# Dilated attention heads: tiles by distance (neighbours in natural order, every fourth token by class) in place of tiles by parity

## The reference, cut to what matters

```python
DILATED_CONFIGS = ((128, 1), (512, 4), (2048, 16))   # (window, dilation)
def dilated_window_branch(q, k, v, slopes, window, dilation):
    # Query t attends keys t + dilation*j, j in [-R, R], R = window // (2*dilation)
    ...
    s = s - slopes[:, None, None] * dist[None]          # dist = |query - key|
    s = jnp.where(valid[None, :, None, None], s, NEG_INF)
    m = jnp.max(s, axis=-1); p = jnp.exp(s - m[..., None]); z = jnp.sum(p, axis=-1)
    ...
wts = jnp.exp(m_all - jnp.max(m_all, axis=0, keepdims=True))
z = jnp.sum(z_all * wts, axis=0)
o_a = jnp.sum(o_all * wts[..., None], axis=0) / z[..., None]
```

## Time and profile before

| | us |
|---|---|
| median of 3 runs | 2054.36 (2050.83 to 2055.28) |
| the profiled execution, its own time | 2054.35 |
| its span, first to last instruction | 2052.6 |
| PE busy | 2016.1 |
| DVE busy | 1211.8 |
| ACT busy | 1129.9 |
| POOL busy | 953.4 |

### The profile page before, as it was taken

The page is one execution under the profiler, slowest core; times in us unless marked ns, Lnnn a source line. Parts: engine busy times, 40 slices in busy tenths (PEclk is TensorE's granted clock), DMA queues, the critical chain, the costliest instruction groups (busy, mean ns, idle before and its releaser), DMA issues.

```text
span 2052.6 us, 25510 instructions
## 1 busy us (share of the span) xinstructions
PE 2016.1 (98%) x9456; PEld 1621.0 (79%) x9456; DVE 1211.8 (59%) x1941; ACT 1129.9 (55%) x1440; POOL 953.4 (46%) x487
## 2 busy tenths in 40 slices
PE   8999998999999999999999999999999999999998
PEld 6788886888888877777887777888777777777888
DVE  6632145325776666673559777414577778776454
ACT  6242234435666666665446444344677778888431
POOL 1222224435555555556102666433566676677401
PEclk9999998999999999999999999999999999999999
DMA  5133478617665754633435333362323343332534
GB/s 203 66 119 126 151 258 310 169 67 155 130 118 109 177 118 93 158 83 122 153 108 163 131 124 116 103 195 78 87 58 85 75 121 74 80 77 90 169 105 167
DMA packets 172143, 261.38 MB, mean 127 GB/s; under 512 B 78754, under 2 KB 89634, under 8 KB 172020
## 3 DMA queue, kind: packets, MB, share of 16 engines
q1 hardware_dynamic: 172020, 259.76, 44.6%
HBM read 161.78 MB, written 97.92 MB: 127 GB/s over the span
## 4 chain that ended last, share of the span: by engine, by line
PE 90%; ACT 3%; DVE 2%; DMA 2%; issue 1%; POOL 1%; SPq 0%; DVEq 0%; ACTq 0%
PE SA L1966 13%; PE OP L2012 11%; PE SM L1892 5%; PE SA L546 5%; PE OP L2019 5%; PE OP L546 5%; PE SM L2065 5%; PE OP L1104 4%; PE SA L2065 4%; PE SA L1104 4%; PE OS L2012 3%; PE OS L546 2%; PE OS L1104 2%; PE OS L2065 2%; PE SM L1888 2%; PE OS L2019 1%
## 5 line engine op out<-in xcount | busy, mean ns | idle before, releaser
L2486 POOL TENSOR_TENSOR c_PL<-c_PF,c_PH 128x1024 fp32r<-128x1024 f32 x128 | 307.7, 2407 | 137.6 <-ACT c_PH L2188 79.9
L2486 POOL TENSOR_TENSOR ab_PL<-ab_PF,ab_PH 128x1024 fp32r<-128x1024 f32 (+3 forms) x128 | 264.7, 2068 | 192.3 <-ACT ab_PH L2188 135.8
L2185 ACT ACTIVATE ab_PF<-SA 128x1024 f32<-128x1024 f32 (+3 forms) x160 | 143.7, 898 | 157.9 <-PE SA L1927 84.7
L2185 ACT ACTIVATE c_PF<-SA 128x1024 f32<-128x1024 f32 x160 | 164.6, 1029 | 84.4 <-PE SA L1966 83.0
L2273 DVE TENSOR_REDUCE c_MH<-SM 128x1 f32<-128x512 f32 x256 | 171.0, 684 | 66.4 <-PE SM L1892 66.3
L437 POOL TENSOR_TENSOR e_wl<-e_raw,e_wh 128x1024 fp32r<-128x1024 f32 (+1 forms) x30 | 70.6, 2354 | 185.1 <-ACT e_wh L613 185.1
L2188 ACT ACTIVATE c_PH<-c_PF 128x1024 fp32r<-128x1024 f32 x128 | 136.0, 1063 | 4.1
L1966 PE MATMUL SA<-c_Q,c_KA 128*128 128x512 f32 x320 | 127.8, 399 | 3.4 <-ACT c_PF L2185 3.4
L1966 PE MATMUL SA<-c_Q,c_KB 72*128 72x512 f32 x320 | 127.1, 397 | 0.0
L1036 POOL TENSOR_TENSOR n_wl<-n_raw,n_wh 128x1024 fp32r<-128x1024 f32 (+1 forms) x24 | 54.5, 2271 | 153.9 <-ACT n_wh L1201 153.9
L1892 PE MATMUL SM<-c_KA,c_Q 128*128 128x512 f32 x320 | 125.1, 392 | 0.0
(11 more groups left out here) (555 smaller groups left out, 5909.5 us busy)
## 6 DMA issues: line engine op xcount, KB each, us to landing
c_Q<-qC_hi SPq DMA_DIRECT2D x32, 384.0 KB, 5.0
e_raw<-in_w_tiles SPq DMA_DIRECT2D x20, 512.0 KB, 4.1
n_raw<-in_w_tiles SPq DMA_DIRECT2D x20, 512.0 KB, 3.7
e_XF<-in_xT SPq DMA_DIRECT2D x12, 512.0 KB, 10.6
silu_gate<-e_ta SPq DMA_DIRECT2D x24, 256.0 KB, 2.0
ab_Q<-qA_hi SPq DMA_DIRECT2D x16, 384.0 KB, 5.4
ab_G<-silu_gate SPq DMA_DIRECT2D x24, 256.0 KB, 3.7
ab_res<-in_xT SPq DMA_DIRECT2D x24, 256.0 KB, 2.9
```

Source lines behind the costliest of these rows:

```text
L2185: nc.scalar.activation(used(PF[p], h, s), used(SA, h, s), ACT.Exp).then_inc(e_done, 1)
L2486: nc.gpsimd.tensor_tensor(used(PL[p], h, s), used(PF[p], h, s), used(PH[p], h, s).bitcast(F32), ALU.subtract).then_inc(p_lo[0], 1)
```

## The change

In a dilated head, keys are held in two kinds of tiles. A class tile has 128 keys of one residue modulo 4 (`class_keys`, `class_queries`: columns of the same `Q1`, `KA`, `Q3`, `KB` buffers with a step of 4 elements, 16 bytes) against all 256 queries of that residue (sample: 128). A near tile has 128 neighbouring keys in natural order against the queries within 64 of them, 192 or 256 columns. A pair is now taken in both tiles if it is held by both kinds of window, so no logarithm is needed, and one bias table of 640 columns in one part does; pairs held by both strided windows are counted by doubling their exponentials on DVE (`doubled`, a product with a table of ones and twos), between the exponential and the copy on ACT. A tile has six score matmuls instead of seven. The values are kept in class order (`VV`) and in natural order (`VN`), low part, high part and ones side by side; the product of a near tile reads `PH` and `PL` with a step of 4 elements, so that the sums stand by class, and for the prompt it is cut in two halves. All copies to `PH` of these heads are ACT's, all subtractions POOL's. The maximum units are 12 a head, of two matmuls and two DVE reductions each; the near maxima are brought into class order by four small matmuls with selection matrices (`pick_max`) and taken together with the class maxima by four small DVE operations (`both_near`), for sample and prompt. The projections store q and k in natural order and the values with 4 KB rows.

```diff
-    def pair_scores(h, s, x, q1, q3, ka, kb):
...
-            nc.tensor.matmul(o, k1, side_of(q1, side, sample), start=True, stop=False, skip_group_check=True)
-            nc.tensor.matmul(o, ident[:], own_bias(Bhi[h % 3], m, n), start=False, stop=False,
-                             skip_group_check=True)
-            nc.tensor.matmul(o[:, l0:l1], ident[:], low, start=False, stop=False, skip_group_check=True)
...
+    def class_keys(t, i):
+        o = i // CLASSES * CH + i % CLASSES
+        return t[:, o:o + CLASSES * (P - 1) + 1:CLASSES]
+
+    def class_queries(t, i, sample):
+        o = SEQ if sample else 0
+        n = (DEC if sample else SEQ) // CLASSES
+        o += i % CLASSES
+        return t[:, o:o + CLASSES * (n - 1) + 1:CLASSES]
...
+            add(c, class_keys(ka, t), class_queries(q1, t, sample), start=True)
+            add(d, tile_keys(ka, i, sample), tile_queries(q1, i, sample))
+            add(c, ident[:], class_bias(Bhi[h % 3], t, sample))
+            add(d, ident[:], near_bias(Bhi[h % 3], i, sample))
+            add(c, class_keys(kb[0:na], t), class_queries(q3[0:na], t, sample), stop=True)
+            return add(d, tile_keys(kb[0:na], i, sample), tile_queries(q3[0:na], i, sample), stop=True)
...
+                nc.tensor.matmul(SM[:, o:o + n], class_keys(q, t), class_queries(k, t, sample), start=True, stop=True)
+                nc.tensor.matmul(SM[:, o + n:o + n + w], tile_keys(q, i, sample), tile_queries(k, i, sample),
+                                 start=True, stop=True).then_inc(m_ready, 1)
...
+                    for b in range(1 if sample else 2):
+                        rs = slice(0, CLASSES) if sample else slice(2 * b, 2 * b + 2)
+                        yield (of_classes(PH[p][:, d])[:, rs], of_classes(PL[p][:, d])[:, rs], near_v,
+                               by_class(out[:])[:, rs, u0:u1], s == 2 and b == 1, False)
...
-            if s not in SLOW_HI:
+            if s not in SLOW_HI or h < NA:
+                if h < NA:
+                    act.wait_ge(p_twice, g + 1)
                 act.wait_ge(e_done, g + 1)
                 nc.scalar.activation(used(PH[p], h, s), used(PF[p], h, s), ACT.Copy).then_inc(p_hi[0], 1)
...
+        def doubled(g):
+
+            h, s, p = g // NS, g % NS, PF[g % 4]
+            dve.wait_ge(e_done, g + 1)
+            if s < 2:
+                x = p[:].rearrange("p (x n) -> p x n", x=2)[:, :, 0:P]
+                count = twice[:, 64:64 + P].unsqueeze(1).to_broadcast([P, 2, P])
+            else:
+                u0 = 64 * ((s - 2) // CLASSES)
+                x, count = p[:, u0:u0 + 192], twice[:, 64 - u0:64 - u0 + 192]
+            nc.vector.tensor_tensor(x, x, count, ALU.mult).then_inc(p_twice, 1)
...
+                for m in range(0, TT, CLASSES):
+                    rows = values[m:m + CLASSES].rearrange("t p d -> (t p) d")
+                    sp.dma_start(VV[b][:, m:m + CLASSES, 0:2 * HD].bitcast(F32),
+                                 rows.rearrange("(u r) d -> u r d", r=CLASSES)).then_inc(in_v[b], 16)
```

More of the change, by code:

```diff
@@ L347, in store @@
                 sp.wait_ge(acc_read, n + 1)
+            if name in ("value", "vB"):
+                for r in (slice(0, HD), slice(HD, P)):
+                    sp.dma_start(S["vA" if name == "value" else "vB"][c, r],
+                                 sv[stage_of(i)][r].rearrange("p h x d -> p h (x d)")).then_inc(stored[stage_of(i)], 16)
+                return
             for part, st in (("hi", sh), ("lo", sl)):
                 src = st[stage_of(i)][rows(n), :]
[L350 to L355, removed]
+                if name == "rope key":
                     dst = S["krB", part][:, cols(c)]
@@ L385, in sync @@
                 sp.wait_ge(tok_ready, 16)
[L386 to L390, removed]
+                sp.dma_start(rtok[:], S["tok0"].rearrange("o (i p) -> (o p) i", p=P),
+                             allow_slow_non_contiguous=True).then_inc(tok_done, 16)
             for w in begins[n]:
@@ L1893, in max_unit, with pick_max @@
                              start=True, stop=True).then_inc(m_ready, 1)
+        def pick_max(h, prompt):
+            pe.wait_ge(m_done, unit0[h + 1] if prompt else unit0[h] + NQ)
+            wait_count(pe, aug_done, 2 * h + prompt)
+            n, o = (NP, 0) if prompt else (NQ, NP)
+            for r in range(CLASSES):
+                mm = nc.tensor.matmul(MT[:, 256 + 8 * r:256 + 8 * r + n], pick[:, r, :], MN[:, o:o + n], start=True,
+                                      stop=True)
+            mm.then_inc(mt_ready, 1)
         def transpose_max(h, prompt):
@@ L2008, in pv @@
             on, n_hi = hi_at[g]
             pe.wait_ge(p_hi[on], n_hi)
-            for pc, kt, out, st, en in halves():
-                for i, (w, r) in enumerate(((vh, P), (vl, HD))):
-                    nc.tensor.matmul(out[0:r], w[:, kt, :], PH[p][:, pc], start=(st and i == 0), stop=False,
-                                     skip_group_check=h < NA)
+            for ph, _, v, out, st, en in halves():
+                for i, (w, r) in enumerate(((v[:, HD:3 * HD], P), (v[:, 0:HD], HD))):
+                    nc.tensor.matmul(out[0:r], w, ph, start=(st and i == 0), stop=False, skip_group_check=h < NA)
@@ L2025, in between @@
                 max_unit(0, u)
+            if NA and g in (sample_at - 1, prompt_at - 1) and part == 2:
+                pe.wait_ge(const_set, n_set)
+                pick_max(0, g == prompt_at - 1)
             if g in (sample_at, prompt_at) and part == 2:
@@ L2033, in tensor @@
             units = units_of(h + 1, s) if h + 1 < NH else ()
-            some = len(units) // 2
+            some = (len(units) + 1) // 2
             scores(h, s)
+            if s in (2, NS - 1) and h + 1 < NA:
+                pick_max(h + 1, s > 2)
             if g >= LAG:
@@ L2377, in vector @@
                 low_part(gate_of(h))
-            if s in SLOW_HI:
+            if h < NA:
+                doubled(g)
+            if s in SLOW_HI and h >= NA:
                 dve.wait_ge(e_done, g + 1)
@@ L2473, in low_weights @@
             nc.gpsimd.tensor_tensor(WL[t][:], WF[t][:], WH[t][:].bitcast(F32), ALU.subtract).then_inc(w_lo, 1)
-        def between(g):
-            if g == MAX0 and NA:
-                bias_low(0)
-        first.main.gpsimd(pool, between)
+        first.main.gpsimd(pool, lambda g: None)
         for g in range(G):
             h, s = g // NS, g % NS
-            if s not in SLOW_LO:
+            if s not in SLOW_LO or h < NA:
                 on, n = hi_at[g]
```

348 lines of the change are left out of this document (184 added, 164 removed).

## The result

| | before | after |
|---|---|---|
| median, us | 2053.48 (2050.83 to 2055.28) | 2073.51 (2072.7 to 2078.39) |
| span of the profiled execution | 2052.6 | 2070.9 |
| PE busy | 2016.1 | 2033.7 |
| DVE busy | 1211.8 | 1215.7 |

The ratio is 1.0102, interval 1.0089 to 1.0114: the changed kernel is 1% slower, 20 us by the medians. The forecast was 2058, within a range of 2022 to 2090. The spans differ by 18.3 us.

The account below looks back on a forecast made before the run. PE, working off its list of matmuls and weight loads, was taken as the bound. From 2054.35 us, 35 gained by the matmuls, 34 lost to stepped reads and 5 to stalls gave 2058, range 2022 to 2090.

Parts of the forecast that it names:

- main case: Dilated heads on PE: stepped moving reads cost 0.22 us per 256-column matmul, stepped weight loads nothing; 2058 us, chance 0.36.
- rival 2: PE's weight loads with the step cost twice too, 3.0 to 3.9 us a head; 2083 us, chance 0.20.
- rival 1: Steps are free on PE, so the gain of 35 us stays, less 13 us of stalls; 2032 us, chance 0.32.
- the gross: PE's matmuls in a dilated head, before steps and stalls: 28.2 to 23.8 us, a gain of 4.4, 35 us in all.
- the moving reads: PE's class queries and near tiles' exponentials, read with a step of 4 elements: 4.3 us a head, 34 us in all.
- the stalls: PE waiting for exponentials held up by the doubling and copy: 0.6 us a head, 5 us in all.
- The load path, which already needs 0.86 ns, would lose nothing: PE's weight loads of class keys, at 0.86 ns a column, pay nothing for the step of 4 elements.
- the prediction's paces: PE's time to the next start: about 0.115 us for 256 columns or less, 0.22 for 256 stepped moving columns.
- Rival 4: ACT and DVE become the bound: 1 to 2 us a head on the main case, 2066 to 2074 us, chance 0.06.
- Rival 2's own sign: Starts on PE after a near score matmul ahead of a class-key load would be 0.22 us apart, not 0.115.

Follow-up runs that it names:

- x_both_plain_writes: `x_both` with DVE's augment and normalise writing plainly instead of with a step of 4, the doubling kept; 2055.43 us, ratio 1.0010.
- x_both: The changed kernel with the step of 4 taken from PE's moving reads and weights, so other pairs are multiplied; 2066.57 us, ratio 1.0067.
- x_no_doubling: The changed kernel without the doubling on DVE and ACT's wait for it, all steps kept; 2068.8 us, ratio 1.0080.
- loose_after: The changed kernel without the doubling and ACT's wait, and with DVE's augment and normalise writing plainly; PE's steps stay; 2069.26 us, ratio 1.0080.
- loose_moving: `loose_after` with the step of 4 also taken from PE's moving reads, the weights keeping theirs; 2048.05 us, ratio 0.9975.
- loose_weights: `loose_after` with the step of 4 also taken from PE's weights, the moving reads keeping theirs; 2051.73 us, ratio 0.9994.
- loose_both: `loose_after` with the step of 4 also taken from PE's moving reads and weights; 2028.38 us, ratio 0.9880.
- x_weights: The changed kernel with the step of 4 taken from PE's weights only, so other pairs are multiplied; 2069.51 us, ratio 1.0077.

## Why the prediction was right or wrong

The time lay in the range, but the likeliest case was not what happened: the verdict is slower, where the main case spread over all three, and the mechanism is that of **rival 2**. A range of 68 us, from rival 1 to rival 2, didn't ask much; and that the forecast missed by 15 us only is in part luck, since the 26 us of the missing term were met by some 12 us of errors the other way (4 in the gross, 6 in the moving reads, 2 in the stalls).

- **"The load path, which already needs 0.86 ns, would lose nothing": this is the step that failed.** Stepped loads take 308 ns instead of 192, and cost 3.3 us a head. Rival 2 had 3.0 to 3.9 for exactly this. The argument compared the paces of two paths and took the slower one to have room for the step already; nothing in the trace said so. The Trainium skill (Advanced Engine Details and Errata, SBUF Cachelines), which names no operand as exempt from its penalty for a new line at each access, was right against it: moving reads, weight loads and DVE's writes all slowed down.
- **The moving reads** cost 3.6 us a head, where the term had 4.3: right mechanism, a fifth too large. Six scores with this step alone took 0.94 us against 0.90 by the prediction's paces; one such matmul takes 0.21 to 0.23 us to the next start, where 0.22 was put.
- **The gross gain** was 4.4 a head and measured 4.9 (28.18 to 23.27): the count of matmuls by the loads' pace held, 23.27 lying between its bare sum of 22.9 and the scaled 23.8.
- **The stalls, 5 us**: PE's loads waited 3.4 us for exponentials, and leaving the doubling out gave 3 by the period, 4.7 by the medians. About right, and for the reason given: PE's steps covered the rest. But a doubling was put at 0.25 to 0.45 us, which holds only for those that meet no subtraction of POOL's; the others took 0.50 to 1.38. This term was left out, and without PE's steps it shows.
- **Rival 1** was priced too well. With no step anywhere but the doubling kept (`x_both_plain_writes`) the time was 2055.4, not 2032: its 1.6 us of stalls a head were 4.1 (27.38 - 23.27), with POOL and the clock in them. **DVE's writes** were taken at their old lengths, which adds 1.7 (29.04 in `x_both`, 2066.6) where PE has no steps; where only the doubling is missing it cost nothing (`x_no_doubling` and `loose_after` have the same period).
- **Rival 4** was a rival only to the main case in the prediction. The measured time lies inside its 2066 to 2074, but the chain isn't what bounds: without it the heads still take 30.00. In fact the chain, 29.0 us a head, lay 1 us under PE's 30.0. Two limits that close explain the three missed expectations: taking the doubling away gives back 0.4 us a head, taking PE's steps away 1.3.
- **"What the new profile would show"**: head to head 28.7, 25.4 or 32 us by case, and 30.38 was measured, between the main case and rival 2. DVE at 20 us a head: 20.8. The waits were to be in slots 5 and 7: most are in slot 7. Rival 2's own sign failed: behind the near matmul that stands ahead of a class-key load the trace has 0.12 us to the next start, not 0.22. The slow load shows behind the class-query matmul instead, 0.23 us with plain moving reads (`loose_moving`) and 0.29 to 0.30 with both steps.

The sum as it should have stood, per head: 4.9 gained, 6.7 for the steps, 0.4 for the doubling (30.38 - 30.00): +2.2, times 8, 17.6 us on the profiled execution's 2054.35 gives 2072; the profiled execution of the changed kernel took 2072.7, the median is 2073.5. Rival 2's 2083 was 11 too high: 4 in the gross, about 6 in the moving reads and 2 in the loads, less 1 in the stalls.

Open: the 1.9 us ahead of the stretch, what makes the clock fall in the first heads, and how much of the chain POOL's subtractions make. A complete kernel without the steps on PE was not tried: it needs keys and queries in both orders, and the near tiles' weights would have to be one run of 128 columns in each. So no version that computes the whole reference beats the kernel before.

## What to carry to other kernels

Fewer columns are not fewer microseconds: this change took 30% of the columns from PE and paid for it in reads with a step of 16 bytes, and it would have paid in DVE's writes next. Price such an access on every operand of every engine (moving reads, weights, writes), or lay the data out in runs first. When an experiment removes the suspected cost and nothing comes back, look for a second limit of nearly the same length, and test the suspect again with that one loosened. And an engine put between two steps of another (here DVE between ACT's exponential and its copy) makes the other stand in its whole queue: price it by what may stand ahead of it and beside it (here POOL's subtraction), not by its own length.

## What the runs showed of the hardware

- A weight load of 128 columns with a step of 16 bytes takes 308 ns, not 192, and a matmul of 256 moving columns with it 0.21 to 0.23 us to the next start where about 0.12 is needed without (`loose_weights`, `loose_both`); a load with a step of 8 bytes was free.
- DVE's writes with that step: 2047 ns instead of 1217 for 64 x 1024, 1098 instead of 678 for 8 x 512.
- A product of two SBUF tiles on DVE (192 columns, 0.33 to 0.36 us by itself) that began while POOL subtracted ended 0.21 to 0.28 us after POOL did, and took up to 1.67 us; all 29 of more than 0.43 us in the changed kernel and all 37 in `x_both` are such.
- After a stall of 4.6 us at full load, PE ran at a granted clock of 0.50 over the next 10 us and 0.65 over the 10 us behind them; with the stall about halved it stayed at 1.00. In `x_no_doubling` it was 0.52 from 480 to 490 us without a stall. Where PE idled in short pieces in every head (`x_both`), a head had 0.94, and such a head took some 1.2 us more than one at 1.00 (`x_weights`).
